# Decay factors of a two-way scan: joined in one VectorE operation, masking moved to ScalarE and GpSimd, one tile later

## What is computed

```
xbc = silu(dwconv(xbc, conv_w, conv_b))            # 24 tiles of 128 channels
a_cs = cumsum(dt * A)                              # per chunk, head, direction
Lm = exp(where(lower, a_cs[l] - a_cs[s], -inf))    # decay from token s to token l
cb = einsum('bclgn,bcsgn->bcgls', Cc, Bc)          # likeness, one matrix per chunk and group
y_diag = einsum('bcgls,bcgrls,bcsgrp->bclgrp', cb, Lm, x * dt)
```

## Time and profile before

| what | value |
|---|---|
| median of 3 runs | 3363.57 us (3356.49 to 3363.72) |
| profiled execution | 3363.13 us, of which the span of the core is 3361.3 us |
| PE busy over the span | 2984.4 us (89%) |
| DVE, ACT, POOL busy | 1257.9, 557.5, 461.4 us (37%, 17%, 14%) |
| stage of the change | from about 546 us to 842.85 us of the span |

### The profile page before, as it was taken

How to read it: one execution, slowest core, us unless ns; L and a number is a source line. 1 busy time by engine, 2 the same in 40 slices (tenths; PEclk the granted TensorE clock), 3 DMA queues, 4 the chain that set the end, 5 groups by cost and what they waited for, 6 DMA issues and landing times. The chain is left out here.

```text
span 3361.3 us, 38535 instructions
## 1 busy us (share of the span) xinstructions
PE 2984.4 (89%) x15902; PEld 1684.8 (50%) x15902; DVE 1257.9 (37%) x2477; ACT 557.5 (17%) x1091; POOL 461.4 (14%) x326
## 2 busy tenths in 40 slices
PE   6997999988999998989999999987978789996995
PEld 5444775555545776534443443434437753544332
DVE  2235844688645444101101101114365553513113
ACT  2001711455012001000000000002023212301111
POOL 0005030254722330000000000001002200002001
PEclk9998999999999998999999999998989899997998
DMA  7722021342312124699999999995110130054996
GB/s 261 257 92 73 2 80 53 123 155 97 113 63 100 50 101 201 272 429 427 428 428 427 427 428 428 428 427 213 38 38 3 36 109 26 26 225 160 425 424 266
DMA packets 141429, 702.30 MB, mean 209 GB/s; under 512 B 18667, under 2 KB 46990, under 8 KB 108233
## 3 DMA queue, kind: packets, MB, share of 16 engines
q1 hardware_dynamic: 124601, 663.80, 49.3%
q10 hardware_dynamic: 11616, 27.92, 2.2%
q0 software_dynamic: 5040, 8.13, 0.7%
HBM read 697.32 MB, written 22.68 MB: 214 GB/s over the span
## 5 line engine op out<-in xcount | busy, mean ns | idle before, releaser
L2353 PE MATMUL ec_wide<-ec_ring,ec_xg 128*64 128x512 f32 x2048 | 456.2, 600 | 19.7 <-issue 15.5
L2353 PEld LDWEIGHTS ec_wide<-ec_ring,ec_xg 128*64 128x64 f32 x2048 | 147.2, 138 | 308.4 <-issue 304.2
L2387 PE MATMUL ec_acc<-ec_ring,ec_hidT 128*64 128x512 f32 x1024 | 232.0, 608 | 30.7 <-DMA ec_ring<-in_w_exp_down 29.9
L2512 DVE TENSOR_SCALAR ec_xg<-ec_piece,ordered 128x128 f32<-128x128 f32 x64 | 21.9, 405 | 567.5 <-PE ec_piece L2401 567.5
L2387 PEld LDWEIGHTS ec_acc<-ec_ring,ec_hidT 128*64 128x64 f32 x1024 | 81.6, 140 | 178.2 <-issue 178.0
L622 POOL TENSOR_TENSOR rkv_sums<-h2mT 128x1024 f32<-128x1024 f32 x2 | 7.0, 3522 | 1000.4 <-DMA uT<-in_x 1000.4
L2401 PEld LDWEIGHTS ec_piece<-ec_sel,x 128*128 128x128 f32 x512 | 122.9, 336 | 8.6 <-issue 5.7
L2401 PE MATMUL ec_piece<-ec_sel,x 128*128 128x128 f32 x512 | 124.4, 406 | 2.8 <-DVE ec_sel L2494 2.8
L4053 PE MATMUL hm_gu<-hm_ring,hm_xg 128*64 128x512 f32 x432 | 115.9, 605 | 5.4 <-DMA hm_ring<-in_moe_w_gu 2.8
L2476 ACT ACTIVATE ec_hidT<-ec_acc 128x512 f32<-128x512 f32 x32 | 17.4, 594 | 518.8 <-PE ec_acc L2376 518.8
L1445 PE MATMUL conv_main<-hT,conv_early 128*128 128x512 f32 x192 | 86.2, 604 | 2.9 <-DVE bcT L1555 2.9
(11 more groups left out here) (795 smaller groups left out, 5392.2 us busy)
## 6 DMA issues: line engine op xcount, KB each, us to landing
ec_ring<-in_w_exp_gate SPq DMA_DIRECT2D x64, 2048.0 KB, 18.0
ec_ring<-in_w_exp_up SPq DMA_DIRECT2D x64, 2048.0 KB, 27.0
ec_ring<-in_w_exp_down SPq DMA_DIRECT2D x64, 2048.0 KB, 19.6
hm_ring<-in_moe_w_gu SPq DMA_DIRECT2D x27, 2048.0 KB, 25.5
hm_ring<-in_moe_w_down SPq DMA_DIRECT2D x11, 2048.0 KB, 28.2
ahead_qkv<-in_w_in SPq DMA_DIRECT2D x10, 2048.0 KB, 9.6
hm_ring_late<-in_moe_w_down SPq DMA_DIRECT2D x5, 2048.0 KB, 24.8
u2T<-in_moe_w_gu SPq DMA_DIRECT2D x5, 2048.0 KB, 22.9
```

The source lines that it names most:

```text
L2353: last = pe.matmul(wide[half(e), b, :], xg[:, u % 2, j, half(e)], w[e][:, a, b * 512:(b + 1) * 512], start=(j == 0), stop=(j == KD - 1))
L2387: last = pe.matmul(acc[half(e), h, :], hidT[:, f, half(e)], w[e][:, r, h * 512:(h + 1) * 512], start=(f == 0), stop=(f == FT - 1))
L2512: last = dve.tensor_scalar(xg[:, u % 2, j, :], piece[:, m % 2, i * P:(i + 1) * P], scale_cols[:, j:j + 1], shift_cols[:, j:j + 1], ALU.mul ...
```

## The change

Falls: ACT copies the row sums out with their sign turned (`scale=-1.0`), so that DVE makes the joined fall of a unit (its negative) in one `scalar_tensor_tensor` per head, from `fall` and from ACT's `back_rows`; `decay` turns the sign back. DVE's `ahead_falls` and POOL's `fall_together` are gone, and `fallen` is now signalled by DVE. Likeness: ACT copies it from PSUM to a new buffer `plain` (`take_alike`), POOL masks it from there, and PE's wait goes to ACT's copy (`alike_taken`). Order: falls come one tile later (`MIX_FIRST` 6), `decay` and `back_falls` stand at the head of ACT's tile, DVE does `share_back(u)` at the end of tile u + 6 behind that tile's falls, and POOL mixes unit u - 1 behind `share_ahead(u)`, except in tiles 9 and 10. SP's code is not touched.

```diff
-MIX_FIRST = 5
+MIX_FIRST = 6
@@ gpsimd
-            def fall_together(u):
-                pool.wait_ge(ahead_fallen, u + 1)
-                pool.wait_ge(back_fallen, u + 1)
-                pool.tensor_tensor(fall[:, u % MIX_ROWS], fall[:, u % MIX_ROWS], back_rows[:, :, :], ALU.subtract).then_inc(fallen, 1)
+            def mask_alike(u):
+                pool.wait_ge(alike_taken, u + 1)
+                if u >= 2:
+                    pool.wait_ge(shared, u - 1)
+                for d, name in enumerate(("upto", "from")):
+                    pool.tensor_tensor(alike[:, u % 2, d], plain[:, u % 2], k.const(name), ALU.mult).then_inc(alike_masked, 1)
...
             for i in range(N_TILES):
-                for u in alike_at(i - 1):
-                    mix(u)
-                for u in falls_at(i):
-                    fall_together(u)
+                behind = len(alike_at(i - 1)) < 2
+                if not behind:
+                    for u in alike_at(i - 1):
+                        mix(u)
                 for u in alike_at(i):
+                    mask_alike(u)
                     share_ahead(u)
+                if behind:
+                    for u in alike_at(i - 1):
+                        mix(u)
@@ tensor
-                        pe.wait_ge(alike_masked, alike_at(i - 1)[-1] + 1)
+                        pe.wait_ge(alike_taken, alike_at(i - 1)[-1] + 1)
@@ scalar
-                act.activation(cumT[:, d, :], bank[0:32, :], ACT.Copy).then_inc(rows_taken, 1)
+                act.activation(cumT[:, d, :], bank[0:32, :], ACT.Copy, scale=-1.0).then_inc(rows_taken, 1)
...
-                act.activation(fall[:, u % MIX_ROWS], fall[:, u % MIX_ROWS], ACT.Exp).then_inc(decayed, 1)
+                act.activation(fall[:, u % MIX_ROWS], fall[:, u % MIX_ROWS], ACT.Exp, scale=-1.0).then_inc(decayed, 1)
+
+            def take_alike(i, n, v):
+                act.wait_ge(alike_ready, alike_at(i)[-1] + 1)
+                if v >= 2:
+                    act.wait_ge(alike_masked, 2 * (v - 1))
+                act.activation(plain[:, v % 2], side[:, (i + 1) % 2, n * P:(n + 1) * P], ACT.Copy).then_inc(alike_taken, 1)
 
             for i in range(N_TILES):
+                for v in falls_at(i - 1):
+                    decay(v)
+                for v in falls_at(i):
+                    back_falls(v)
                 silu(i)
+                for n_at, v in enumerate(alike_at(i)):
+                    take_alike(i, n_at, v)
+                silu_c(i)
                 if i > R:
                     take(i - 1)
-                for v in falls_at(i):
-                    back_falls(v)
-                for v in falls_at(i - 1):
-                    decay(v)
@@ vector
+            def falls(u):
                 c, g = u // SSD_G, u % SSD_G
                 dve.wait_ge(rows_loaded[u % MIX_ROWS], 16 * (u // MIX_ROWS + 1))
+                dve.wait_ge(back_fallen, u + 1)
                 for h in range(HG):
-                    ins = dve.tensor_scalar(fall[:, u % MIX_ROWS, h, :], fall[:, u % MIX_ROWS, h, :], cum[:, c, g * HG + h:g * HG + h + 1], 0.0,
-                                            ALU.subtract, ALU.min)
-                ins.then_inc(ahead_fallen, 1)
...
+                    ins = dve.scalar_tensor_tensor(fall[:, u % MIX_ROWS, h, :], fall[:, u % MIX_ROWS, h, :], cum[:, c, g * HG + h:g * HG + h + 1],
+                                                   back_rows[:, h, :], ALU.add, ALU.max)
+                ins.then_inc(fallen, 1)
...
                 conv_main(i)
-                for v in alike_at(i - 1):
-                    share_back(v)
-                for n_at, v in enumerate(alike_at(i)):
-                    mask_alike(i, n_at * P, v)
                 conv_side(i)
                 for v in falls_at(i):
-                    ahead_falls(v)
+                    falls(v)
+                for v in alike_at(i):
+                    share_back(v)
```

More of the change, by code:

```diff
@@ L1301, in steps_and_conv @@
         alike = work[:, 1, 4 * CTX:4 * CTX + 4 * P].rearrange("p (b d l) -> p b d l", d=2, l=P)
+        plain = work[:, 1, 4 * CTX + 4 * P:4 * CTX + 6 * P].rearrange("p (b l) -> p b l", l=P)
         cum = a[:, :, :].rearrange("p t h -> p (t h)").rearrange("p (m h) -> p m h", h=SSD_H)
         rows_loaded = [sem(f"rows_loaded{b}") for b in range(MIX_ROWS)]
-        back_loaded, ahead_fallen, back_fallen, fallen, decayed = (sem(x) for x in ("back_loaded", "ahead_fallen", "back_fallen", "fallen", "decayed"))
+        back_loaded, back_fallen, fallen, decayed = (sem(x) for x in ("back_loaded", "back_fallen", "fallen", "decayed"))
+        alike_taken = sem("alike_taken")
         alike_ready, alike_masked, ahead_shared, shared, mixed = (sem(x) for x in ("alike_ready", "alike_masked", "ahead_shared", "shared", "mixed"))
@@ L1376, in _ @@
         def _(pool):
-            def fall_together(u):
-                pool.wait_ge(ahead_fallen, u + 1)
-                pool.wait_ge(back_fallen, u + 1)
-                pool.tensor_tensor(fall[:, u % MIX_ROWS], fall[:, u % MIX_ROWS], back_rows[:, :, :], ALU.subtract).then_inc(fallen, 1)
+            def mask_alike(u):
[4 more added lines that the diff above has]
+                    pool.tensor_tensor(alike[:, u % 2, d], plain[:, u % 2], k.const(name), ALU.mult).then_inc(alike_masked, 1)
             def share_ahead(u):
                 c, g = u // SSD_G, u % SSD_G
-                pool.wait_ge(alike_masked, u + 1)
+                pool.wait_ge(alike_masked, 2 * (u + 1))
                 if u >= 2:
@@ L1490, in silu, with silu_c @@
                 act.activation(convolved(i), convolved(i), ACT.Silu, bias=b).then_inc(silued, 1)
+            def silu_c(i):
                 if i >= R:
+                    b = vec[:, V_CONVB + CONV_TILES[i]:V_CONVB + CONV_TILES[i] + 1]
                     act.wait_ge(side_taken, i - R + 1)
@@ L1525, in back_falls @@
                 for h in range(HG):
-                    ins = act.activation(back_rows[:, h, :], back_rows[:, h, :], ACT.Relu, scale=-1.0,
+                    ins = act.activation(back_rows[:, h, :], back_rows[:, h, :], ACT.Relu,
                                          bias=cum[:, N_SEG + c, g * HG + h:g * HG + h + 1])
@@ L1592, in _ @@
             dve.tensor_scalar(a[:, :, :], a[:, :, :], -1.0, None, ALU.mult).then_inc(a_ready, 1)
-            def ahead_falls(u):
+            def falls(u):
                 c, g = u // SSD_G, u % SSD_G
                 dve.wait_ge(rows_loaded[u % MIX_ROWS], 16 * (u // MIX_ROWS + 1))
+                dve.wait_ge(back_fallen, u + 1)
                 for h in range(HG):
-                    ins = dve.tensor_scalar(fall[:, u % MIX_ROWS, h, :], fall[:, u % MIX_ROWS, h, :], cum[:, c, g * HG + h:g * HG + h + 1], 0.0,
-                                            ALU.subtract, ALU.min)
-                ins.then_inc(ahead_fallen, 1)
[L1601 to L1607, removed]
+                    ins = dve.scalar_tensor_tensor(fall[:, u % MIX_ROWS, h, :], fall[:, u % MIX_ROWS, h, :], cum[:, c, g * HG + h:g * HG + h + 1],
+                                                   back_rows[:, h, :], ALU.add, ALU.max)
+                ins.then_inc(fallen, 1)
             def share_back(u):
```

## The result

The changed kernel takes 3445.42 us, the median of 4 runs (3441.65 to 3447.59), against 3363.09 us before. The ratio is 1.0252, with a 95% interval of 1.0239 to 1.0264: 82 us slower. The forecast was 3446. In the comparisons further down three executions (4246.81 us in run 5, 6083.48 us in run 7, 6084.18 us of the kernel before) belong to a slower state, and neither the times given nor the ratios count them.

What follows compares the result with a forecast made beforehand. No engine was full; a ring through ACT, POOL and DVE set 13.1 us a tile. Taps and falls 8.4, store wait 7.7, mix 2.3 and share_back 2.1 made 20.5: 83 us more, 3446 us, range 3405 to 3468.

Steps and rivals of the forecast that it cites:

- The wait for the store: Between DVE's falls and share_back: the store, issued behind a load, lands, then share_ahead runs; 7.7 us a tile.
- The mix's turn: Behind share_ahead, POOL's mix runs before DVE's share_back and shuts it out; 2.3 us a tile.
- The rival without it (3421): share_back starts before or beside the mix; tiles 9 and 11 to 20 each lose 2.3 us: 3421, chance 0.22.
- Tile by tile: Changed stage from tile 8 to its end, summed by tile: 292.2 us, the stage ending 83 us later.
- POOL's masks: Two likeness masks a tile move to POOL; 0.4 us each by size, at most 1.9.
- One sign was counted twice: Signs of being right: DVE idle about 10 us ahead of share_back, first L1626 of each tile some 2.3 us.
- ACT's copy: ACT copies the likeness from PSUM in each tile; at most 0.37 us.
- PE's lower clock: PE idles some 8.5 us a tile, so a side product takes 3 us more; priced at nothing except in the tail.
- The slower rival: PE stays at 1.2 GHz, 22.4 us a tile, or masks of 1.9 us each cost as much: 3467, chance 0.07.
- The faster rival: The store is out before the falls, DVE needs 10.5 us against PE's 11.2, PE's waits go: 3334, chance 0.04.

Runs made afterwards that it cites:

- run 5: run 4 with DVE's falls put between main and side taps: 3338.86 us, ratio 0.9940 to the kernel before.
- run 7: The kernel before with the likeness part of the change alone (ACT copies, POOL masks, PE waits for the copy): 3366.28 us, ratio 1.0016.
- run 1: The changed kernel with SP's store of a unit put ahead of its load of backward rows: 3375.42 us, ratio 1.0057 to the kernel before.
- run 2: The changed kernel with the falls a tile earlier (MIX_FIRST 5), nothing else: 3377.29 us, ratio 1.0060 to the kernel before.
- run 3: The changed kernel with POOL's mix at the head of its tile in all tiles: 3422.92 us, ratio 1.0193 to the kernel before.
- run 4: The changed kernel with the edits of run 1 and run 3 together: 3358.38 us, ratio 1.0001 to the kernel before.
- SP by tiles: run 5 with SP's queue in tile order (stores and rows, next backward rows, weight load): 3337.12 us, ratio 0.9930 to the kernel before.
- run 8: SP by tiles with the likeness part taken back, DVE masking from PSUM behind its main taps: 3346.49 us, ratio 0.9956 to the kernel before.

## Why the prediction was right

*The wait for the store* was the main term, and it holds as written: a wait of 7.7 us between falls and `share_back`, 7.96 in the tile shown. Runs 1 and 2 remove it from two sides, and 65 us with it.

*The mix's turn*, 2.3 us a tile, measured 2.05 by run 3. The rival without it (3421) is out. The trace puts it at 4.25 us for 8 operations instead of 2.19 in each tile from 11 to 20; no row tells what decided the 0.08 us between the engines.

*Tile by tile*, predicted and measured: tile 8 17.9 and 16.6; tile 9 22.1 and 21.9; tile 10 18.2 and 18.3; tiles 11 to 20 204.6 and 204.7; the rest 29.4 and 28.8. In sum 292.2 and 290.3. In tile 8 POOL's masks, counted at 1.6 us, ran among DVE's falls, which took 6.2 us against 2.1 of their own and 3.8 for two `share_ahead`. The profiled execution (3441.65 us) lies 4 us under the forecast: 2 are in these tiles, 3.4 ahead of the stage, and 0.6 comes back behind it (83.3 had been rounded to 83). That the median came within 1 us of 3446 is in part luck: the four executions spread over 6 us. The store landed after 5.5 us in the tile shown, where I had taken the 5.3 of the earlier trace rows.

*One sign was counted twice.* DVE was to idle about 10 us ahead of `share_back`, and the first L1626 to take some 2.3 us; both hold the mix's turn. The trace has 7.96 us idle and a first operation of up to 2.43.

*POOL's masks* took 0.41 us each, as assumed; ACT's copy 0.26, under its bound of 0.37.

*PE's lower clock* is there in each tile (a side product of 6.66 us at 753.66, and 0.83 as the mean) and costs nothing, as priced: DVE waits for PE once in the stage's tiles, 2.5 us ahead of the first. The idle piece before that product was 6.2 us, not the 8.5 of the prediction; in the tile shown it was 5.6 and the product took 5.20. The slower rival, in which it sets the pace, did not come.

*The faster rival* turned on the store coming ahead of the falls. Runs 1 and 4 make it so and reach 3375 and 3358, not 3334: I had taken DVE's 10.5 us against PE's 11.2 as all that was left. The turns with POOL and the ring through the one buffer of backward rows were missing in that rival. Only with the falls ahead of the side taps does PE set the pace, at 3339, and 3337 with SP by tiles.

## What to carry to other kernels

A diff that moves the work which signals a semaphore moves every DMA that is queued behind the wait on it. Follow each signal that changes its sender into the issuing queue, and read what stands behind that wait, even where the queue's own code is untouched. Where two engines shut each other out, sum a tile for both of them with their turns, and prefer an order in which each long operation of the one lies under an operation of the other that doesn't collide. A large wait of the busiest engine is no price list: taking away the thing it waits for only shows the next one in the ring. And where two engines drift apart, read a tile's length at the one that never waits: in run 5 DVE's starts said 10.8 us and PE's 11.2.

## What the hardware showed beside this

Which engine gets its turn is not settled by the first start of a run of operations. In the kernel before, a mix that started behind the first of DVE's 8 operations ended only 2.36 us, its usual time, after all 8 were over (4235 ns). In run 8 `share_ahead`, 0.16 us behind the first fall, took its 1.94 us at once, and DVE's second operation lasted 1.98 us. In tile 8 of the changed kernel a fall that began 0.01 us ahead of `share_ahead` (638.13 against 638.14) still took 2.05 us. Why these differ stays open.
